# State-space mixer: conv features by 512-column matmuls, halves summed by ScalarE and VectorE into SBUF

## The reference, cut to what matters

```python
def mamba2_mixer(h, w_in, conv_w, conv_b, dt_bias, a_log, d_skip, norm_w, w_out):
    proj = h @ w_in
    z = proj[..., :D_INNER]
    xbc = proj[..., D_INNER:D_INNER + CONV_DIM]       # 4096 features: 2048 of x, 1024 of B, 1024 of C
    dt = proj[..., D_INNER + CONV_DIM:]
    xbc = jax.nn.silu(causal_depthwise_conv(xbc, conv_w, conv_b))    # 4 taps along time
    ...
    y = ssd_chunked(xs, dt, a, bm, cm)
    ...
```

## Time and profile before

| | |
|---|---|
| median of 3 runs | 1723.66 us (1723.4 to 1723.74) |
| the profiled execution | 1723.25 us, its span 1721.5 us |
| TensorE, weight loads | busy 1708.5 us, 1480.4 us |
| VectorE, ScalarE, GpSimd | busy 1198.7, 873.9, 116.7 us |
| granted TensorE clock | 0.999 of 2.4 GHz |
| mean transfer rate | 173 GB/s |
| the conv stage in the trace | blocks 1 to 15 from 214.45 to 303.66 us |

### The profile page before, as it was taken

One profiled execution on the slowest core, in us unless ns is written; L12 is line 12 of the kernel. 1 busy time (PEld: TensorE's weight loads), 2 busy tenths in 40 slices (PEclk: granted clock), 3 DMA queues, 4 the chain that ended last, 5 costly groups with the idle time before them and its releaser, 6 DMA issues.

```text
span 1721.5 us, 24764 instructions
## 1 busy us (share of the span) xinstructions
PE 1708.5 (99%) x9466; PEld 1480.4 (86%) x9466; DVE 1198.7 (70%) x1391; ACT 873.9 (51%) x1100; POOL 116.7 (7%) x158
## 2 busy tenths in 40 slices
PE   9999999999999999999999999999999999999998
PEld 7888899888888888889888888988887888888887
DVE  7667799675776777667767767876557665577676
ACT  5434586764443454436864444765337634454343
POOL 0000031140000000002500000110000100000000
PEclk9999999999999999999999999999999999999999
DMA  7564465334646555563336455554554454445643
GB/s 257 189 204 166 153 213 172 123 119 132 220 167 218 175 192 185 180 207 108 122 123 220 168 197 188 171 196 147 185 183 146 156 188 146 171 155 200 208 165 114
DMA packets 215424, 298.26 MB, mean 173 GB/s; under 512 B 13557, under 2 KB 171322, under 8 KB 215354
## 3 DMA queue, kind: packets, MB, share of 16 engines
q1 hardware_dynamic: 215290, 297.27, 51.7%
q10 hardware_dynamic: 64, 0.02, 0.0%
HBM read 296.21 MB, written 1.05 MB: 173 GB/s over the span
## 4 chain that ended last, share of the span: by engine, by line
PE 97%; DVE 1%; ACT 1%; DMA 0%; issue 0%; SPq 0%; DVEq 0%; POOL 0%; ACTq 0%
PE PS L474 27%; PE PS L480 14%; PE PS L349 12%; PE PS L350 12%; PE PS L426 7%; PE PS L368 5%; PE PS L461 2%; PE PS L466 2%; PE PS L462 2%; PE PS L343 1%; PE PS L345 1%; PE PS L344 1%; PE PS L1142 1%; PE PS L774 1%; PE PS L2135 0%; PE PS L398 0%
## 5 line engine op out<-in xcount | busy, mean ns | idle before, releaser
L327 ACT ACTIVATE whi<-raw 128x2048 fp32r<-128x2048 f32 (+3 forms) x286 | 534.5, 1870 | 460.6 <-PE PS L480 371.6
L332 DVE TENSOR_TENSOR wlo<-raw,whi 128x2048 fp32r<-128x2048 f32 (+3 forms) x286 | 635.5, 2238 | 123.5 <-ACT whi L327 123.2
L474 PE MATMUL PS<-XT,whi 128*128 128x512 f32 x2016 | 471.9, 390 | 2.1 <-DVE XT L889 1.9
L474 PEld LDWEIGHTS PS<-XT,whi 128*128 128x128 f32 x2016 | 376.2, 188 | 80.3 <-issue 3.3
L480 PEld LDWEIGHTS PS<-XT,wlo 128*128 128x128 f32 x2016 | 252.1, 191 | 5.9
L480 PE MATMUL PS<-XT,wlo 128*128 128x256 f32 x2016 | 255.0, 283 | 0.0
L705 DVE TENSOR_REDUCE ff_s<-PS 128x512 f32<-128x1024 f32 x55 | 67.4, 1225 | 207.7 <-PE PS L480 200.0
L350 PE MATMUL PS<-whi,aT 128*128 128x512 f32 x400 | 156.3, 391 | 0.0
L349 PE MATMUL PS<-whi,aT 128*128 128x512 f32 x400 | 156.2, 390 | 0.0
L349 PE MATMUL PS<-whi,XT 128*128 128x512 f32 (+2 forms) x320 | 125.6, 394 | 0.1
L350 PE MATMUL PS<-whi,XT 128*128 128x512 f32 (+2 forms) x320 | 122.1, 383 | 0.0
(11 more groups left out here) (446 smaller groups left out, 2185.2 us busy)
## 6 DMA issues: line engine op xcount, KB each, us to landing
raw<-in_w_in SPq DMA_DIRECT2D x112, 512.0 KB, 4.5
raw<-in_ffn_w_up SPq DMA_DIRECT2D x88, 512.0 KB, 5.1
raw<-in_ffn_w_down SPq DMA_DIRECT2D x88, 512.0 KB, 4.3
raw<-in_ffn_w_gate SPq DMA_DIRECT2D x86, 512.0 KB, 4.4
raw<-in_ssm_w_in SPq DMA_DIRECT2D x48, 512.0 KB, 4.6
raw<-in_w_ffn_in SPq DMA_DIRECT2D x44, 512.0 KB, 4.3
raw<-in_w_ffn_out SPq DMA_DIRECT2D x22, 512.0 KB, 4.3
raw<-in_ssm_w_out SPq DMA_DIRECT2D x16, 512.0 KB, 4.1
```

The lines of the kernel that those rows point to most:

```text
L327: act.activation(whi[s][:, 0:size], raw[s][:, 0:size], ACT.Copy).then_inc(hi_done, 1)
L332: dve.tensor_tensor(wlo[s][:, 0:size], raw[s][:, 0:size], whi[s][:, 0:size].bitcast(FP32), ALU.subtract).then_inc(lo_done, 1)
L474: return pe.matmul(o, whi[n % SLOTS][:, sl], XT[:, k, :, :].rearrange("p a n -> p (a n)"), start=(k == 0), stop=False)
```

## The change

Blocks 1 to 14 (`SUMMED`) are made by `mul_pairs` into two banks each: banks 0 and 1 for odd blocks, 2 and 3 for even ones. ScalarE copies the low products of both halves to SBUF (`ff_s` or `ff_a`, in turn), VectorE adds the high ones from PSUM onto them, and the last tap (ScalarE) and the other three (VectorE) read that sum from SBUF. Blocks 0 and 15 stay as they are, block 15 in bank 0. TensorE's waits change with the banks: block 2 waits for the taps of block 0, block `i` from 3 on for the sum of block `i - 2`.

```diff
@@ new helpers, and TensorE (ssm_pe)
+        SUMMED = range(1, NXB - 1)
+        sums = (ff_s, ff_a)
+        def both_banks(i):
+            return PS[:, 0:2, :] if i % 2 else PS[:, 2:4, :]
+        def xbc(i):
+            if i in SUMMED:
+                return sums[i % 2]
+            return features(0) if i == 0 else psD[:, 0, :].rearrange("p (c n) -> p c n", c=2)
+        def xbc_ready(i):
+            return (A["sum"], i) if i in SUMMED else (block_used, (N["bc"] + i if i else N["bc0"]) + 1)
...
-                        pe.wait_ge(*((A["z"], q) if q > 1 else (A["tap"], 14)))
+                        pe.wait_ge(*((A["z"], q) if q > 1 else (A["sum"], 14)))
...
+                    if i == 2:
+                        pe.wait_ge(A["tap"], 1)
                     if i >= 3:
-                        pe.wait_ge(A["tap"], max(i - 3, 1))
-                    mul_features(pe, nx + i, psD[:, FEATURE_BANK[i % 4], :])
+                        pe.wait_ge(A["sum"], i - 2)
+                    if i in SUMMED:
+                        mul_pairs(pe, nx + i, both_banks(i))
+                    else:
+                        mul_features(pe, nx + i, psD[:, 0, :])
@@ ScalarE (ssm_act; conv_act now takes the wait and the source as arguments)
+                if i in SUMMED:
+                    act.wait_ge(block_used, nx + i + 1)
+                    if i >= 3:
+                        act.wait_ge(A["tap"], i - 1)
+                    act.activation(sums[i % 2][:, :, :], both_banks(i)[:, :, SEQ:2 * SEQ], ACT.Copy).then_inc(A["half"], 1)
+                conv_act(act, A, i, xbc_ready(i) if i < NXB else None, xbc, xbc_tiles(i) if i < NXB else None, ssm_taps,
...
@@ VectorE (ssm_dve)
             for i in range(NXB):
+                if i in SUMMED:
+                    dve.wait_ge(A["half"], i)
+                    dve.tensor_tensor(sums[i % 2][:, :, :], both_banks(i)[:, :, 0:SEQ], sums[i % 2][:, :, :], ALU.add)\
+                       .then_inc(A["sum"], 1)
                 lo_upto(dve, at, nx + i + 2)
-                conv_dve(dve, own, A, i, xbc_tiles(i), ssm_taps)
+                if i in SUMMED:
+                    dve.wait_ge(A["sum"], i)
+                conv_dve(dve, own, A, i, xbc, xbc_tiles(i), ssm_taps)
```

More of the change, by code:

```diff
@@ L1043, in build @@
         ssm_ctx.close()
-        A = sems("ssm", "in xb e dq dt dta dtN coln acc tap silu turned nat z b masked e_done m dx y y_added yz sq var r gs "
+        A = sems("ssm", "in xb e dq dt dta dtN coln half sum acc tap silu turned nat z b masked e_done m dx y y_added yz sq var r gs "
                         "gt gh gl")
         NXB = 16
+        SUMMED = range(1, NXB - 1)
+        sums = (ff_s, ff_a)
         def y_cross(g):
@@ L1178, in ssm_pe, with conv_act @@
                     mul_out(pe, no + g, 0, left, g == 0, False)
-        def conv_act(act, S, i, n, tiles, taps, bias, prev):
-            if n is not None:
-                act.wait_ge(block_used, n + 1)
+        def conv_act(act, S, i, ready, source, tiles, taps, bias, prev):
+            if ready is not None:
+                act.wait_ge(*ready)
                 if i >= 2:
@@ L1186, in conv_act @@
                 for c in range(2):
-                    m = act.activation(conv_acc[:, i % 2, c, :], features(i)[:, c, :], ACT.Identity,
+                    m = act.activation(conv_acc[:, i % 2, c, :], source(i)[:, c, :], ACT.Identity,
                                        scale=taps(tiles[c], CONV_K - 1), bias=bias(tiles[c]))
@@ L1192, in conv_act, with conv_dve @@
                 act.activation(prev, conv_acc[:, (i - 1) % 2, :, :], ACT.Silu).then_inc(S["silu"], 1)
-        def conv_dve(dve, own, S, i, tiles, taps):
+        def conv_dve(dve, own, S, i, source, tiles, taps):
             dve.wait_ge(S["acc"], i + 1)
@@ L1200, in conv_dve @@
                     a = conv_acc[:, i % 2, c, sh:SEQ]
-                    m = dve.scalar_tensor_tensor(out=a, in0=features(i)[:, c, 0:SEQ - sh],
+                    m = dve.scalar_tensor_tensor(out=a, in0=source(i)[:, c, 0:SEQ - sh],
                                                  scalar=taps(tiles[c], j), in1=a, op0=ALU.mult, op1=ALU.add)
@@ L1242, in ssm_act @@
                         act.wait_ge(A["turned"], i - 9 - 2)
-                conv_act(act, A, i, (nx + i if i else N["bc0"]) if i < NXB else None, xbc_tiles(i) if i < NXB else None, ssm_taps,
+                if i in SUMMED:
[4 more added lines that the diff above has]
+                conv_act(act, A, i, xbc_ready(i) if i < NXB else None, xbc, xbc_tiles(i) if i < NXB else None, ssm_taps,
                          lambda ct: cols[0][:, 80 + ct:81 + ct], prev)
@@ L2365, in b2_act @@
                     act.activation(lsum[:, :], lsum[:, :], ACT.Exp).then_inc(B["lam"], 1)
-                conv_act(act, B, i, (n + i if i else N["mqk0"]) if i < 8 else None, (2 * i, 2 * i + 1), b2_taps,
+                conv_act(act, B, i, (block_used, (n + i if i else N["mqk0"]) + 1) if i < 8 else None, features,
+                         (2 * i, 2 * i + 1), b2_taps,
                          lambda ct: 0.0, QK[:, 2 * (i - 1):2 * i, :] if i else None)
@@ L2551, in b2_dve @@
                 lo_upto(dve, at, N["mqk"] + i + 2)
-                conv_dve(dve, own, B, i, (2 * i, 2 * i + 1), b2_taps)
+                conv_dve(dve, own, B, i, features, (2 * i, 2 * i + 1), b2_taps)
                 if i == 2:
```

## The result

The changed kernel takes **1739.16 us** (median of 4 runs, 1738.18 to 1739.40), the kernel before 1723.62 in the same runs: a ratio of 1.0089, 95% interval 1.0077 to 1.0101. That is slower by 15.5 us where 9.8 were forecast: 2.7 us above the forecast's own range (to 1736.5) and 0.7 us above the widest one (to 1738.5). The profiled execution took 1739.08 us, its span 1737.4.

A forecast was written before the change was run, and what follows sets the result against it. TensorE, busy for 99% of the span, was taken to bound the kernel. Added waits of 12.5 us less 2.7 of shorter blocks gave +9.8, so 1723.25 became 1733.05; with 0.4 for the median, 1733.5 us, range 1731 to 1736.5.

The forecast's parts named there:

- The sign: Whole kernel: slower was given 0.92, within 0.2% 0.06, faster 0.02.
- Gain on TensorE: 14 conv blocks with fewer, wider matmuls: 0.20 us less a block, 2.7 us counted in all.
- No other gain: Whole change: the shorter TensorE blocks are all it can win, 0.16% of the time.
- Sum: VectorE, conv stage: 14 added sums of 128x512 at 0.60 us of line, 8.4 us in all.
- the walk: Hand count of the TensorE, VectorE and ScalarE queues through blocks 0 to 15; it put the decay scores 9.8 us later.
- Taps: VectorE, conv blocks: six taps reading SBUF instead of PSUM stay at 2.59 us a block, no gain.
- an upper bound: VectorE's taps at 2.80 us a block if GpSimd's work slows two SBUF operands: +12.6 us.
- The stall of 2.5 us at block 2: TensorE before block 2, which takes block 0's banks, waits 2.5 us for block 0's taps.
- The long wait before block 15: TensorE behind block 14 waits 4.0 us, since 5.06 us of rotary tables stand before block 13's sum.
- The clock, rival 3: TensorE's clock drops to 1.2 GHz for block 15 after the wait: +14.1 us, 1737.6; chance 6%.
- The second rival: Conv stage: VectorE does the sums in spare time, TensorE keeps its 2.7 us, 1720.9 us; chance 8%.
- the first: VectorE's taps from SBUF fall to 2.27 us a block: +5.9 us, 1729.6; chance 14%.

The follow-up runs named there:

- the short sum: The changed kernel with VectorE's sum cut to 8 columns of each half, all waits and copies kept: 1732.42 us.
- half of the blocks: The change made in blocks 1 to 7 only, blocks 8 to 15 as in the kernel before: 1731.84 us.
- three edits together: The changed kernel with GpSimd's x-block work held back, block 2 in banks 4 and 5, and the rotary tables behind the last taps: 1730.78 us.

## Why the prediction was wrong in size

The sign, the mechanism and most terms held; the time was out of the range because one term was sized wrong, the taps beside GpSimd. The forecast also put the clock at nothing, which is worth under 1 us.

- **Gain on TensorE, 0.20 us a block**: held (5.57 a block). **No other gain**: held.
- **Sum, 0.60 us of line each, 8.4 in all**: held (222.76 to 223.36); without nearly all of it 6.7 us come off, where the walk had 5.0.
- **Taps, "2.59 us a block as now"**: this is the step that failed. Alone the taps are as forecast, 2.61 of line; beside GpSimd six took up to 4.24. The prediction had the mechanism as an upper bound ("if two SBUF operands suffer when GpSimd works beside them") but spread it as 2.80 over all blocks, a number without a row behind it, when the question was how much in which blocks. In sum 2.80 everywhere would have been 2.9 us; it was 5.3, of which 3.1 in blocks 11 and 12, right before the tables. With GpSimd away from these two the time fell by 3.7 us, which alone brings it into the forecast's own range; the 2.2 us of blocks 4 and 5 were never taken away by themselves, and that they cost as much is the walk's account. The Trainium skill has the rule: by its page "SBUF — State Buffer" (SBUF: two separate sides) VectorE with two SBUF inputs and a GpSimd instruction that reads SBUF exclude each other for a whole instruction. The runs agree for GpSimd instructions with two reads (a tap up to 0.96 us instead of 0.48) and for the splits, which GpSimd waits out (3.12 instead of 0.85). Between the short taps and GpSimd instructions with one read they don't: a tap takes 0.62 at most, and neither side waits for the whole of the other.
- **The stall of 2.5 us at block 2**: held in size. The prediction called it "as good as the whole gain, before anything else"; its removal was worth 0.2 us, nothing that can be told from the spread, since VectorE is behind anyway.
- **The long wait before block 15, forecast 4.0**: 5.1; with the two slow sets of taps that stand right before it gone, 2.9. The tables' 5.06 us as the cause: held, 4.8 came off by the median, with the one longer execution named above.
- **The clock, rival 3**: given 6%, and it did fall, at two places, to 1.2 GHz (0.50 in the window from 311.24 to 315.00). But the price of +4.3 us was too high: block 15 with its transposes took 1.9 us longer and not 5.76, and the time gained by keeping the clock up there comes back as a wait for VectorE. "No trace here shows such a fall" was a misreading: in the trace of the kernel before, the clock is 0.50 from 1718.00 to 1720.00, behind TensorE's last matmul at 1715.12. The Trainium skill's warning against idle gaps stands in the page "TensorE: Matmul & The Clock Gate" under "Why this matters for your kernels"; the falls here agree with it. And +14.1 on 1723.66 is 1737.8, not 1737.6.
- **The second rival (not slower)** and the first (cheaper taps): nothing speaks for them; 2.70 us for six from SBUF against 2.68 from PSUM.
- **The walk**: with the measured tap times it gives +16.0 for +15.5, and for the nine kernels timed in rounds it was within 0.8 us of the median in seven; it was 1.6 too short for the sum in PSUM and 1.8 too long for the short sum, and neither miss is resolved. The walk had the changed kernel's measured durations in it by then, so this tests the order of the queues and not the prices of the prediction.

## What to carry to other kernels

When a change moves an operand of a VectorE instruction from PSUM to SBUF, price it by the instruction's own duration only where GpSimd is idle; look up in GpSimd's timeline what runs beside it, and count up to double where an instruction there reads two tiles. Before giving an engine more work to relieve TensorE, add up its line through the stage, one-off pieces included, and ask who waits for each of them: here 8.4 us of sums went to a queue with 6 us to spare, for 2.7 us of matmuls. And a stall of the busiest engine costs its length only if no other queue is late behind it: 2.5 us taken away here moved the median by 0.2.

## What the runs showed of the hardware that was not expected

- A VectorE instruction on 128x256 with both operands in SBUF takes 0.48 us alone and up to 0.96 beside GpSimd instructions that read two tiles (most taps of blocks 11 and 12: 0.71 to 0.83); beside memsets 0.48, beside instructions that read one 0.47 to 0.62. With one operand in PSUM it takes 0.48 beside all of them.
- It is not one-sided: GpSimd's product of 128x256 took 0.77 us beside such taps, about 0.6 beside taps from PSUM, and an instruction of 0.85 us took 3.12 beside a split of 2.27.
- VectorE instructions with one SBUF tile to read are not spared: four `tensor_scalar` of 32x256 (L1358) took 1.74 us instead of 1.12, three of them beside GpSimd's `tensor_scalar` in the changed kernel with idle GpSimd work.
- The granted clock fell to half behind TensorE waits of 2.5 and 5.1 us in the changed kernel, and behind waits of 1.85 to 1.90 us in four others (tables behind the taps, TensorE kept busy, half of the blocks, idle GpSimd work). It stayed at 1.00 behind 2.35 us (tables behind the taps), 2.65 us (half of the blocks) and 1.87 us (three edits together). So the length of a wait alone does not decide it, and what does these runs don't tell. The windows of block 2 and of block 8 with the tables behind the taps:

```profile
223.00:226.00 3.00, 3.00 (x14) 2.47 (x15) 3.00 (x4) 2.57 (x4) 0.63 (x1) 1.00 0.33 116
259.50:261.50 2.00, 2.00 (x6) 1.58 (x5) 2.00 (x3) 2.00 (x3) 0.00 (x0) 0.50 0.00 0
```
